# Wider value products, values ahead of keys, and a closer timetable of attention heads in a two-block transformer kernel

## What is computed

```python
# first block
h = x + hybrid_mixer(rmsnorm(x, norm_mix))      # state-space heads (ssd), short conv (sc), w_out
h = h + memory_cross_attention(rmsnorm(h, norm_xa), rmsnorm(mem, mem_norm))   # xa, 4 heads
h = h + swiglu(rmsnorm(h, norm_ffn))            # 44 x 128 wide
x2 = rmsnorm(h, norm_final)
# second block
q_a,k_a,v_a, q_b,k_b,v_b, q_c,k_c,v_c = split(rmsnorm(x2, attn_norm) @ w_qkv)
y_a = rmsnorm(softmax1(q_a k_a) - lam * softmax2(q_a k_a)) @ v_a   # 8 differential heads of 128
y_b = stick_breaking(q_b, k_b, v_b)             # 8 heads of 64, two in a task
y_c = chunk_band(q_c, k_c, v_c)                 # 8 heads of 64, two in a task
x3 = x2 + concat(y_a, y_b, y_c) @ w_o
out = rmsnorm(x3 + gated_conv_ffn(rmsnorm(x3)))
```

## Time and profile before

| | us |
|---|---|
| median of 3 runs | 2786.58 (2786.55 to 2788.6) |
| the profiled execution | 2785.78 |
| its span | 2784.0 |
| TensorE busy | 2749.0 (99%) |
| VectorE busy | 1946.7 (70%) |
| ScalarE busy | 1289.3 (46%) |
| GpSimd busy | 86.6 (3%) |
| records of TensorE products | 16612 |

### The profile page before, as it was taken

The page is one execution under the profiler, slowest core; times in us unless marked ns, Lnnn a source line. Parts: engine busy times, 40 slices in busy tenths (PEclk is TensorE's granted clock), DMA queues, the critical chain, the costliest instruction groups (busy, mean ns, idle before and its releaser), DMA issues.

```text
span 2784.0 us, 40021 instructions
## 1 busy us (share of the span) xinstructions
PE 2749.0 (99%) x16612; PEld 2423.5 (87%) x16612; DVE 1946.7 (70%) x2382; ACT 1289.3 (46%) x1650; POOL 86.6 (3%) x61
## 2 busy tenths in 40 slices
PE   8999999999999999999999999999999999999997
PEld 7888998888898888888888889888988888888886
DVE  7777778766768665666566776775777757765775
ACT  5444546754545443444344545554444433433444
POOL 1000000002001000000000110000100000000001
PEclk9999999999999999999999999999999999999999
DMA  6555554456555555555555554443555655555553
GB/s 241 183 187 185 175 172 158 145 164 212 177 167 186 194 191 190 185 195 190 189 188 192 181 182 154 153 155 122 174 174 182 202 184 181 188 190 188 184 188 122
DMA packets 138197, 499.14 MB, mean 179 GB/s; under 512 B 15248, under 2 KB 16280, under 8 KB 137888
## 3 DMA queue, kind: packets, MB, share of 16 engines
q1 hardware_dynamic: 136224, 491.67, 53.5%
q10 hardware_dynamic: 1792, 4.91, 0.5%
HBM read 494.41 MB, written 2.11 MB: 178 GB/s over the span
## 4 chain that ended last, share of the span: by engine, by line
PE 96%; DVE 3%; ACT 1%; issue 0%; DMA 0%; DVEq 0%; ACTq 0%
PE PS L477 95%; DVE wlo L1216 1%; ACT whi L819 1%; DVE XG L1416 0%; DVE XG L1653 0%; DMA XG<-in_x 0%; DVE AR L1525 0%; DVE AR L1226 0%; DVE XG L1199 0%; PE PS L560 0%; PE PS L716 0%; ACT AR L1069 0%; DVE XG L1651 0%; DVE H L1210 0%; PE PS L638 0%
## 5 line engine op out<-in xcount | busy, mean ns | idle before, releaser
L477 PE MATMUL PS<-H,whi 128*128 128x512 f32 (+1 forms) x5472 | 1798.0, 381 | 9.0 <-DVE wlo L1681 8.1
L1216 DVE TENSOR_TENSOR wlo<-raw,whi 128x1024 fp32r<-128x1024 f32 x929 | 1128.7, 1229 | 674.7 <-ACT whi L819 669.7
L477 PE MATMUL PS<-H,wlo 128*128 128x256 f32 x5072 | 1423.7, 281 | 0.0
L819 ACT ACTIVATE whi<-raw 128x1024 fp32r<-128x1024 f32 x929 | 969.8, 1057 | 979.2 <-PE PS L477 958.3
L477 PEld LDWEIGHTS PS<-H,whi 128*128 128x128 f32 x5472 | 1002.3, 188 | 220.8 <-DVE H L1210 8.0
L477 PEld LDWEIGHTS PS<-H,wlo 128*128 128x128 f32 x5072 | 960.9, 189 | 2.0 <-issue 1.7
L477 PE MATMUL PS<-Y,whi 128*128 128x512 f32 (+1 forms) x2240 | 724.2, 378 | 1.1 <-DVE XG L1653 0.8
L477 PE MATMUL PS<-Y,wlo 128*128 128x256 f32 x2048 | 575.0, 281 | 0.0
L477 PEld LDWEIGHTS PS<-Y,whi 128*128 128x128 f32 x2240 | 408.3, 188 | 85.0 <-DVE XG L1653 2.0
L477 PEld LDWEIGHTS PS<-Y,wlo 128*128 128x128 f32 x2048 | 388.2, 190 | 0.2
L1525 DVE TENSOR_REDUCE AR<-PS 128x512 f32<-128x1024 f32 x140 | 171.5, 1225 | 14.9 <-PE PS L477 0.5
(11 more groups left out here) (168 smaller groups left out, 914.5 us busy)
## 6 DMA issues: line engine op xcount, KB each, us to landing
raw<-in_ffn SPq DMA_DIRECT2D x528, 512.0 KB, 4.3
raw<-in_w_in SPq DMA_DIRECT2D x177, 512.0 KB, 4.6
raw<-in_w_qkv SPq DMA_DIRECT2D x96, 512.0 KB, 3.8
raw<-in_w_out SPq DMA_DIRECT2D x64, 512.0 KB, 4.2
raw<-in_w_o SPq DMA_DIRECT2D x40, 512.0 KB, 3.8
raw<-in_w_q SPq DMA_DIRECT2D x8, 512.0 KB, 3.9
raw<-in_w_k SPq DMA_DIRECT2D x8, 512.0 KB, 3.9
raw<-in_w_v SPq DMA_DIRECT2D x8, 512.0 KB, 4.1
```

What stands on the lines that cost most here:

```text
L477: return e.matmul(out, l, r, start=start, stop=stop)
L819: a.then_inc(e.activation(c.whi[:, s % NW, :], c.raw[:, s % NRAW, :], ACT.Copy), "whi")
L1216: v.then_inc(e.tensor_tensor(c.wlo[:, s % NW, :], c.raw[:, s % NRAW, :], c.whi[:, s % NW, :].bitcast(F32), ALU.subtract), "wlo")
```

## The change

- The 512-column values: `va`, `vb`, `vc` take four blocks at a time (2, 1 and 1 tiles instead of 4, 2 and 2), `wide` lays their weights out accordingly, and `values` copies 512 columns twice. `wv` stays at two blocks.
- Order of tiles: `qa`, `va`, `ka`, `qb`, `vb`, `kb`, and `qc`, `kc`, `vc`. `dfa` waits for the keys of its own head only. `ao2` walks its first tile with the two columns side by side.
- Timetable: `dfa` starts 8 slots after `ka` has begun and every 7, with its transposes 5 slots behind the scores instead of 9; `dfb` 10 slots behind `dfa` instead of 13; `stk` and `bnd` have shorter distances too (the numbers in `BANKS` are slots from a task's start). `ssd` starts two slots later.
- In ScalarE's and VectorE's loops the side step comes first in a slot, ahead of `split` and `leave`.
- Norm sums are one product of 512 columns; `mean2` on VectorE adds the two halves. The column sums go; instead the finished row (`RMB`, `RN`) is turned into two columns by two products (`column`, tasks `mcol` and `rcol`), which VectorE copies.
- Group norms: GpSimd adds the four squares into one tile of 256 columns (two additions), and TensorE sums with one product instead of four; root and output come two slots later.

The diff, without the waits' shorter distances in `stk` and `bnd`, which follow the same pattern, and without declarations and the layout on the host:

```diff
@@ -68,7 +69,7 @@
 def walk(stage, j, K, m):
...
-    if stage in ("su", "xo") and j == 0:
+    if stage in ("su", "xo", "ao2") and j == 0:
@@ -90,8 +91,9 @@
-            for name, n in (("qa", 4), ("ka", 4), ("va", 4), ("qb", 2), ("kb", 2), ("vb", 2), ("qc", 2), ("kc", 2), ("vc", 2)):
-                out += [(name, j, "H", 0, 16, 2) for j in range(n)]
+            for name, n, m in (("qa", 4, 2), ("va", 2, 4), ("ka", 4, 2), ("qb", 2, 2), ("vb", 1, 4), ("kb", 2, 2), ("qc", 2, 2),
+                               ("kc", 2, 2), ("vc", 1, 4)):
+                out += [(name, j, "H", 0, 16, m) for j in range(n)]
@@ -168,21 +170,21 @@
-    out += [(z + 2 + 4 * i, "ssd", i) for i in range(16)]
+    out += [(z + 4 + 4 * i, "ssd", i) for i in range(16)]
...
-    out += [(first_slot("wo2") + 14, "msq", 0), (first_slot("wo2") + 32, "mnorm", 0)]
+    out += [(first_slot("wo2") + 14, "msq", 0), (first_slot("wo2") + 32, "mnorm", 0), (first_slot("wo2") + 38, "mcol", 0)]
...
-    out += [(a + 4, "norm", 3), (a + 6, "mid", 0), (a + 28, "norm", 4), (a + 32, "qa", 0)]
-    v = after("ka")
-    out += [(v + 7 * h, "dfa", h) for h in range(8)]
-    out += [(v + 7 * h + 13, "dfb", h) for h in range(8)]
-    out += [(v + s, "stk", i) for i, s in enumerate((57, 71, 85, 99))]
-    out += [(v + s, "bnd", i) for i, s in enumerate((105, 114, 124, 136))]
+    out += [(a + 4, "norm", 3), (a + 6, "mid", 0), (a + 28, "norm", 4), (a + 32, "qa", 0), (a + 35, "rcol", 0)]
+    v = first_slot("ka")
+    out += [(v + 8 + 7 * h, "dfa", h) for h in range(8)]
+    out += [(v + 18 + 7 * h, "dfb", h) for h in range(8)]
+    out += [(v + s, "stk", i) for i, s in enumerate((71, 84, 97, 110))]
+    out += [(v + s, "bnd", i) for i, s in enumerate((119, 128, 136, 144))]
@@ -214,19 +216,21 @@
+    "mcol": [("b", 0, 2, "mcol_ok", 1, 1)],
+    "rcol": [("b", 0, 2, "rcol_ok", 1, 1)],
...
-    "grp": [("b", 4, 5, "grp_root", 1, 1)],
+    "grp": [("b", 5, 7, "grp_root", 1, 1)],
...
-    "dfa": [("s0", 2, 6, "dif_exp", 2, 1), ("s1", 2, 6, "dif_exp", 2, 2), ("t", 11, 12, "dif_copy", 1, 1)],
-    "dfb": [("o", 0, 6, "dif_y", 1, 1), ("n", 2, 4, "dif_root", 1, 1)],
-    "stk": [("s0", 2, 4, "stk_q", 2, 1), ("s1", 2, 4, "stk_q", 2, 2), ("c0", 12, 14, "stk_z", 2, 1),
-            ("c1", 12, 14, "stk_z", 2, 2), ("o", 19, 25, "stk_y", 1, 1), ("n", 21, 23, "stk_root", 1, 1)],
-    "bnd": [("s0", 2, 5, "bnd_exp", 2, 1), ("s1", 2, 5, "bnd_exp", 2, 2), ("t0", 10, 12, "bnd_copy", 2, 1),
-            ("t1", 10, 12, "bnd_copy", 2, 2), ("o", 14, 20, "bnd_y", 1, 1), ("n", 16, 18, "bnd_root", 1, 1)],
+    "dfa": [("s0", 2, 5, "dif_exp", 2, 1), ("s1", 2, 5, "dif_exp", 2, 2), ("t", 7, 8, "dif_copy", 1, 1)],
+    "dfb": [("o", 0, 4, "dif_y", 1, 1), ("n", 1, 3, "dif_root", 1, 1)],
+    "stk": [("s0", 2, 4, "stk_q", 2, 1), ("s1", 2, 4, "stk_q", 2, 2), ("c0", 10, 12, "stk_z", 2, 1),
+            ("c1", 10, 12, "stk_z", 2, 2), ("o", 16, 20, "stk_y", 1, 1), ("n", 17, 19, "stk_root", 1, 1)],
+    "bnd": [("s0", 2, 5, "bnd_exp", 2, 1), ("s1", 2, 5, "bnd_exp", 2, 2), ("t0", 8, 10, "bnd_copy", 2, 1),
+            ("t1", 8, 10, "bnd_copy", 2, 2), ("o", 11, 15, "bnd_y", 1, 1), ("n", 12, 14, "bnd_root", 1, 1)],
@@ -483,33 +485,42 @@
-    def norm_mm(bank, s, start, stop, cols):
-        mm(bank[:, 0:T], c.ones, s[:, 0:T], start, False)
-        last = mm(bank[:, 0:T], c.ones, s[:, T:2 * T], False, stop)
-        if cols:
-            for i in range(2):
-                o = bank[:, T + i:T + i + 1]
-                mm(o, s[:, i * P:(i + 1) * P], c.ones[:, 0:1], True, False)
-                last = mm(o, s[:, T + i * P:T + (i + 1) * P], c.ones[:, 0:1], False, True)
-        return last
+    def column(kind, i, row, ready, n, name):
...
+        bank = take(kind, i, "b")
+        p.wait_ge(ready, n)
+        mm(bank[:, 0:1], row[:, 0:P], c.ident[:, 0:1], True, True)
+        p.then_inc(mm(bank[:, 1:2], row[:, P:T], c.ident[:, 0:1], True, True), name)
...
     def norm(n):
...
-        last = norm_mm(bank, c.SUM, True, n != 6, n in (3, 4))
-        if n == 6:
+        if n < 6:
+            last = mm(bank, c.ones, c.SUM, True, True)
+        else:
+            mm(bank[:, 0:T], c.ones, c.SUM[:, 0:T], True, False)
+            mm(bank[:, 0:T], c.ones, c.SUM[:, T:2 * T], False, False)
...
-            last = norm_mm(bank, c.SQ[1], False, True, False)
+            mm(bank[:, 0:T], c.ones, c.SQ[1][:, 0:T], False, False)
+            last = mm(bank[:, 0:T], c.ones, c.SQ[1][:, T:2 * T], False, True)
...
+        yield
...
+    def mcol(_):
+        column("mcol", 0, c.RMB, "mnorm_ok", 1, "mcol_turn")
+        yield
...
+    def rcol(_):
+        column("rcol", 0, c.RN, "rr", 1, "rcol_turn")
...
     def mnorm(_):
...
-        p.then_inc(norm_mm(bank, c.MSUM, True, True, True), "mnorm_sum")
+        p.then_inc(mm(bank, c.ones, c.MSUM, True, True), "mnorm_sum")
...
     def sc(j):
@@ -582,12 +593,10 @@
     def grp(g):
-        yield from idle(4)
+        yield from idle(5)
...
-        p.wait_ge("grp_sq", g + 1)
-        for n in range(4):
-            last = mm(bank[:, 0:T], c.ones, c.grp_q[n // 2][:, (n % 2) * T:(n % 2 + 1) * T], n == 0, n == 3)
-        p.then_inc(last, "grp_sum")
+        p.wait_ge("grp_add", g + 1)
+        p.then_inc(mm(bank[:, 0:T], c.ones, c.grp_q[0][:, 0:T], True, True), "grp_sum")
...
     def xa(h):
@@ -619,7 +628,7 @@
-        p.wait_ge("qk", 16)
+        p.wait_ge("qk", 10 + 2 * (h // 2))
@@ -630,7 +639,7 @@
-        yield from idle(9)
+        yield from idle(5)
@@ -643,10 +652,10 @@
-        p.wait_ge(*done("va", h // 2))
+        p.wait_ge(*done("va", h // 4))
...
-        yield from idle(2)
+        yield from idle(1)
@@ -763,14 +772,14 @@
-                wh, wl = halves(b, 2)
+                wh, wl = halves(b, m)
...
-                    out, start = c.acc[n][:, t, 0:T], k == k0
+                    out, start = c.acc[n][:, t, 0:m * P], k == k0
...
-                b = finish(b, 2, last)
+                b = finish(b, m, last)
@@ -988,7 +994,7 @@
     def dfa(h):
...
-        yield from idle(5)
+        yield from idle(4)
@@ -1002,7 +1008,7 @@
-        yield from idle(6)
+        yield from idle(4)
@@ -1011,11 +1017,11 @@
-        yield from idle(3)
+        yield from idle(2)
...
-        yield from idle(3)
+        yield from idle(2)
@@ -1091,8 +1097,9 @@
+        w = P * GEMM[NUM[stage, j]][5]
...
-            ins = e.activation(dst[:, m * n + j * T:m * n + (j + 1) * T], c.acc[b][:, m, 0:T], ACT.Copy,
+            ins = e.activation(dst[:, m * n + j * w:m * n + (j + 1) * w], c.acc[b][:, m, 0:w], ACT.Copy,
@@ -1176,11 +1183,11 @@
+        side.step(t)
...
-        side.step(t)
@@ -1229,6 +1236,12 @@
+    def mean2(m, bank, eps, name):
...
+        v.then_inc(e.tensor_scalar(m, bank[:, 0:T], 1.0 / 2048, eps, ALU.mult, ALU.add))
+        v.wait_ge(*v.at)
+        v.then_inc(e.scalar_tensor_tensor(m, bank[:, T:2 * T], 1.0 / 2048, m, ALU.mult, ALU.add), name)
@@ -1419,8 +1428,19 @@
-        v.then_inc(e.tensor_tensor(c.RN, c.RN, c.RN2, ALU.mult))
-        v.then_inc(e.tensor_tensor(c.ucol, c.ucol, c.ucol2, ALU.mult), "rr")
+        v.then_inc(e.tensor_tensor(c.RN, c.RN, c.RN2, ALU.mult), "rr")
+        yield
...
+    def mcol(_):
+        yield
+        v.wait_ge("mcol_turn", 1)
+        v.then_inc(e.tensor_copy(c.mcol, c.bank("mcol", 0, "b")[:, 0:2]), "mcol_ok")
+        yield
...
+    def rcol(_):
+        yield
+        v.wait_ge("rcol_turn", 1)
+        v.then_inc(e.tensor_copy(c.ucol, c.bank("rcol", 0, "b")[:, 0:2]), "rcol_ok")
...
     def dfa(h):
@@ -1451,7 +1471,7 @@
     def dfb(h):
...
-        yield from idle(5)
+        yield from idle(3)
@@ -1731,7 +1751,17 @@
-    side = Side({"sqx": sqx, "msq": msq, "mid": mid})
+    def grp(k):
...
+        q0, q1 = c.grp_q
+        yield
+        g.wait_ge("grp_sq", k + 1)
+        g.then_inc(e.tensor_tensor(q0, q0, q1, ALU.add))
+        g.wait_ge(*g.at)
+        g.then_inc(e.tensor_tensor(q0[:, 0:T], q0[:, 0:T], q0[:, T:2 * T], ALU.add), "grp_add")
+        yield
...
+    side = Side({"sqx": sqx, "msq": msq, "mid": mid, "grp": grp})
```

More of the change, by code:

```diff
@@ L737, in done @@
         return f"acc{b}", n + 1
-    side = Side({"norm": norm, "mnorm": mnorm, "sc": sc, "cb": cb, "dt": dt, "xs": xs, "ssd": ssd, "grp": grp, "xa": xa,
-                 "dfa": dfa, "dfb": dfb, "stk": stk, "bnd": bnd})
+    side = Side({"norm": norm, "mnorm": mnorm, "mcol": mcol, "rcol": rcol, "sc": sc, "cb": cb, "dt": dt, "xs": xs, "ssd": ssd,
+                 "grp": grp, "xa": xa, "dfa": dfa, "dfb": dfb, "stk": stk, "bnd": bnd})
     b = 0
```

96 lines of the change are left out of this document (44 added, 52 removed).

## The result

In the first set of executions the change brought the median from 2787.08 us (11 executions, 2785.24 to 2802.5) to 2766.79 us (11 executions, 2762.13 to 2780.11), ratio 0.9934 with the interval 0.9913 to 0.9954. The same two kernels in another set, later in the study: before 2776.25 us (19 executions), after 2778.23 us (12), ratio 0.9992 (0.9974 to 1.0011). My forecast was 2778 us and 8.7 us less. How one change can be worth 20 us and nothing is the main thing to explain here.

What follows compares the result with a forecast made beforehand. TensorE's issued products and its waits bound the kernel. Products -9.6, old waits -9.6, new waits +9.7, side-work order +0.8 us: -8.7, so 2778 us from the median 2786.6; 8-in-10 range 2767 to 2784.

Steps and rivals of the forecast that it cites:

- Wide values: Second attention's values: 768 products of 256 columns become 384 of 512 on TensorE, 2.6 us saved.
- Column sums: Norm 3, norm 4 and mnorm: one-column products go, two column calls come, 1.8 us saved.
- Norm sums, nothing: One 512-column norm product instead of two of 256 saves nothing, between 0 and 0.02 us.
- Group squares: Group norms: four fp32 products become one, four times, 5.2 us saved; GpSimd's adds hidden with 3 us to spare.
- The timetable: Attention stage: old waits of 9.6 us go, shorter new ones of 9.7 us come at five heads and two stk.
- rival C: Attention waits pile up to 13 to 18 us, clock falls behind waits above 2.7 us; 2781 to 2786, chance 0.20.
- Rival B: Closer attention timetable holds without waits, so the 9.7 us don't come; 2768 us (2765 to 2774), chance 0.20.
- Side work first: Side steps ahead of split and leave: scores sum 0 some 1.5 us later, small gains elsewhere; net 0.8 us lost.
- `mid`: Stage where VectorE releases a qa tile's bank 0.8 us late; without column roots some 0.6 us earlier.
- `ssd` 0: Two slots later, clear of the last xs convolution but before the last silu; 0.2 us gain taken.
- Rival D: Waiting side steps delay split, so TensorE waits for wlo weight halves; slower, mostly 2787 to 2800, chance 0.10.

Runs made afterwards that it cites:

- a_narrow: Changed kernel with the second attention's values in products of 256 columns again; 9 executions at 2769.9 us, 1 at 2783.3.
- b_norm512: Kernel before with only norm sums 0, 1, 2 and 5 as one 512-column product each; median 2785.73 us.
- a_norm256: Changed kernel with norm sums 0 to 5 and the memory's again two 256-column products; median 2779.37 us.
- a_far: Changed kernel with a stretched timetable: heads' transposes seven slots behind scores, later attentions two slots later, group sums one; 2 executions at 2757.7 us, 4 at 2772.9.
- a_best2: a_best with scores sum 0 one slot later; median 2759.65 us, ratio to before 0.9903.
- a_sidelast: Changed kernel with split and leave ahead of side work again on ScalarE and VectorE; median 2790.65 us.
- a_best: a_far with stk 3 and the bnd at old slots, side work first only in group sums and from second attention on; median 2750.08 us, ratio to before 0.9875.
- b_grp: Kernel before with only the group squares added on GpSimd, one product per group; 5 executions at 2768.1 us, 6 at 2781.8, 1 at 2794.2.

## Why the prediction was right or wrong

**Total.** At equal levels the gain is 8.9 to 9.6 us, forecast 8.7. Taken against the one-fast-part level on which the shown times of before lie (2786.6), 2778 us is the changed kernel's middle level, 2778.3. The median of the first set, 2766.8, lies 11 us lower, 0.2 us below the range's lower end, since 6 of its 11 executions had both parts fast and none of before's did. I treated the stream's interval as a constant; the earlier trace rows are from before's fast part, and the second part of the same trace already ran at 353.2 ns. Reading one more row there would have shown the 14 us.

**Wide values, 2.6 us.** Mis-sized; 4.7 by the trace, 5.0 to 5.3 by a_narrow. The step that failed is the long product's price: 0.232 us, taken from its place in a block beside a short one, where it is 0.2267 behind its like.

**Column sums, 1.8 us.** Holds. The four one-column records of `mcol` show 0.58 us in all, start to start of what is around them 0.56 more than a block without them; `rcol` adds 0.37. 2.7 went and 0.93 came.

**Norm sums, nothing.** Holds as a cost of its own (b_norm512 and a_norm256 keep their kernels' levels).

**Group squares, 5.2 us, hidden.** The products' part holds; the cover does not at the fourth group. TensorE waits there for 1.2 us, which delays it 1.35. Timeline of the changed kernel:

```profile
600.44 0.63 ACT L944 ACTIVATE AR<-AR 128x512 f32<-128x512 f32 x1 [3.66 <-DVE AR L1361]
...
600.97 0.62 ACT L942 ACTIVATE AR<-AR 128x512 f32<-128x512 f32 x1
...
601.67 1.29 POOL L1759 TENSOR_TENSOR AR<-AR 128x512 f32<-128x512 f32 x1 [13.30 <-ACT AR L942]
...
603.04 1.05 POOL L1761 TENSOR_TENSOR AR<-AR 128x256 f32<-128x256 f32 x1
```

The adds are as long as priced (2.34 us, forecast 2.4 to 3.0). But ScalarE's squares stood idle for 3.66 us until VectorE's last `ssd` multiply (L1361), behind residual adds. I had counted the 3 us of spare from the squares' slot, and the squares of this group aren't in their slot.

**The timetable, 9.6 go and 9.7 come.** The old waits are gone. The new ones, as delay to the next product:

| | head 1 | head 3 | head 4 | head 5 | head 7 | stk 0 | stk 2 | sum |
|---|---|---|---|---|---|---|---|---|
| forecast | 0.5 | 2.15 | 1.0 | 2.6 | 0.5 | 2.1 | 0.8 | 9.7 |
| measured | 0.40 | 1.95 | 0.92 | 2.56 | 0.41 | 2.47 | 0.89 | 9.6 |

Each is where it was forecast and none is elsewhere. Head 3 in the changed kernel, in the order of the forecast's sum (split, weights, transposes):

```profile
1750.56 1.23 DVE L1223 TENSOR_TENSOR wlo<-raw,whi 128x1024 fp32r<-128x1024 f32 x1 [2.01 <-ACT whi L828]
...
1751.70 0.17 DVE L1459 RECIPROCAL AR<-AR 128x4 f32<-128x4 f32 x1
...
1752.89 0.75 DVE L1468 SCALAR_TENSOR_TENSOR AR<-AR 128x128 f32<-128x128 f32 x2
...
1753.78 0.52 PE L647 MATMUL PS<-AR 128*128 128x128 f32 x3 [1.79 <-DVE AR L1468]
```

What the table leaves out is the clock. Behind head 5's wait of 2.41 us it fell, and so it did behind the 2.81 us at scores sum 0; columns as in the windows above:

```profile
59.40:63.40 4.00, 4.00 (x14) 0.57 0.64 199
1783.50:1787.00 3.50, 3.50 (x10) 0.53 0.47 147
```

Five blocks from 60.25 to 63.42 take 3.17 us where 1.73 is normal, and eight 512-column products from 1783.52 to 1786.79 take 3.27 where 1.81 is: 1.4 and 1.5 us lost. My sum had no such term; only rival C had, and there for waits above 2.7 us. No such bound holds: in the changed kernel's second profile the clock also fell behind waits of 2.05 (scores sum 0, 0.72 from 56 to 62 us) and 2.41 us (`stk` 0), while behind `stk` 0's 2.40 us in the first it stayed at 1.00.

Rival B (no waits) is refuted by these, and so are rival C's 13 to 18 us of waits: with head 5's clock they come to 11.1. a_far and a_best2 show the other half: these waits were a lack of distance and nothing else, since with two slots more the heads' went and none returned there.

**Side work first, 0.8 us lost.** The sign holds before the second attention and the size doesn't. Scores sum 0 went from 0.70 us of delay to 2.97, 2.3 more where 1.5 was forecast. The named cause is there, VectorE's newton late behind ScalarE's split:

```profile
46.04 1.22 DVE L1223 TENSOR_TENSOR wlo<-raw,whi 128x1024 fp32r<-128x1024 f32 x1 [1.89 <-ACT whi L828]
47.19 0.42 DVE L1248 SCALAR_TENSOR_TENSOR AR<-AR 128x256 f32<-128x256 f32 x1
```

It isn't the whole: with split and leave first the wait is still 1.5 us (a_sidelast) and 1.7 (a_best). It also varies: the kernel before and those made from it show 0.5 to 1.0 us there, the traces with side work first and this sum at its old slot 1.9 to 2.8.

`mid` gained 0.3 us (0.97 to 0.65), not 0.6; `ssd` 0 nothing (1.21 to 1.24), not 0.2. Two I didn't name: norm 1 lost 0.9 us (L1734, GpSimd's squares added later: 1.26 us from the last block's second product to the norm's, it was 0.37) and the first memory head 0.4. In a_best, where split and leave come first in those stages, they are gone. What I missed most is what the reordering is for: a_sidelast shows 25 us that it holds off.

**Rival D** (a waiting side step makes weight halves late, slower) didn't come: beside the start TensorE waits for `wlo` only at 13.1 and 30.5 us, 0.24 and 0.47, and nowhere in the attention stage.

**The account.** -4.7 - 1.8 - 5.2 from the products, 9.6 - 9.6 from the timetable, +2.3 + 0.9 + 0.4 - 0.3 from the order and +1.35 at the group: 7.1 us less. To that come 1.5 us at 30 to 34 us (the short waits behind the start), 2.9 for the two falls of the clock, -0.4 at the start (the first block earlier, the clock up sooner) and -2.9 for the short stretches: outside the two parts, blocks that nothing interrupts took 8.8 us more in before than they would at 346.7 ns, and 5.8 in the changed kernel. The sum is 6.0 us less, and the two profiled executions, each with one fast part, differ by 5.7. Each of them is off its level's median, before's 1.4 us below, the changed kernel's 1.8 above, which is why the levels differ by 9. Over the profiles that stretch term is 8.2 to 8.8 us in the kernel before and the two with a changed norm product, 5.3 in b_grp and 3.9 to 6.5 in the ten with the whole change or most of it. So some 3 us of the level's gain may be the rate of short stretches and not work saved; one or two profiles of a kernel can't say how much. My sum came out at 8.7, near the levels, partly by luck: 2.1 us too little for the wide values stand against 3.9 too little for the waits named above that lie outside attention, the 4.4 us of short waits and clock that had no term at all, and stretch rates that I didn't know of.

## What to carry to other kernels

When times lie on levels, sort the executions by level first and compare level with level; a median over a mixture moved by 20 us and by nothing for a change that moved each level by 9. Within a level the rates of short stretches and falls of the clock still differ by a few us from execution to execution. Count a stream's records in equal windows at several places before taking its interval as a constant. For a timetable written out in slots, walk through each step's distance with the durations of the trace: that found seven waits to within 0.4 us each, and giving late steps one or two slots more, with the order of side work chosen stage by stage, brought another 17 us.

## What the hardware showed that I hadn't expected

- TensorE streams the same pair of products (512 and 256 columns) at 346.5 or 353.2 ns a block, at a granted clock of 1.00 in both, for over 700 us at a time. Start to start over a whole part it is 346.7 and 353.3, in periods of the 2.4 GHz clock 832 and 848. The slow rate has a cycle of three blocks.
- The rate comes out anew in each execution, in the short stretches too, and its odds differ between sets (the kernel before had 26 to 79% of its feed-forward parts fast) and between kernels of one set (15 of 58 and 21 of 24). Two parts make 28 us between the best and the worst execution of one program.
- 512-column products behind one another start 0.2267 us apart, less than the 0.23 to 0.24 of the long product in a mixed pair. The Trainium skill, TensorE: Matmul & The Clock Gate, Back-to-back issue gap, gives 518 cycles for 512 columns as the gap of an isolated product, 0.216 us at 2.4 GHz; the trace is longer in both places.
- The granted clock fell behind single waits of TensorE of 2.05, 2.41 and 2.81 us and stayed at 1.00 behind others of 2.23 (a_narrow, head 5) and 2.40 us. The two falls in the changed kernel's first profile cost 1.4 and 1.5 us.
